# RWKV-7 scan on one core: the triangular inverse on 64x64 diagonal blocks, its last level as corner products, and the tail by four heads

## What is computed

```python
def step(S, inp):
    r_t, w_t, k_t, v_t, kk_t, b_t = inp
    sa = jnp.einsum('bhvk,bhk->bhv', S, -kk_t)
    S = (S * w_t[:, :, None, :] + sa[..., None] * b_t[:, :, None, :]
         + v_t[..., None] * k_t[:, :, None, :])
    y_t = jnp.einsum('bhvk,bhk->bhv', S, r_t)
    return S, y_t
_, y = lax.scan(step, S0, ...)      # 16 heads of 64, 256 steps
```

## Time and profile before

| | us |
|---|---|
| median of three runs | 1625.1 |
| the profiled execution, its own time | 1619.88 |
| its span, first to last instruction | 1618.0 |
| TensorE busy (8756 matmul records) | 1531.3 |
| VectorE busy | 1007.7 |
| ScalarE busy | 684.1 |
| POOL busy | 40.7 |
| mean granted TensorE clock | 0.979 |

### The profile page before, as it was taken

One profiled execution on the slowest core, in us unless ns is written; L12 is line 12 of the kernel. 1 busy time (PEld: TensorE's weight loads), 2 busy tenths in 40 slices (PEclk: granted clock), 3 DMA queues, 4 the chain that ended last, 5 costly groups with the idle time before them and its releaser, 6 DMA issues.

```text
span 1618.0 us, 20860 instructions
## 1 busy us (share of the span) xinstructions
PE 1531.3 (95%) x8756; PEld 1321.3 (82%) x8756; DVE 1007.7 (62%) x1384; ACT 684.1 (42%) x957; POOL 40.7 (3%) x48
## 2 busy tenths in 40 slices
PE   5998998889999989999999999999999999899998
PEld 5777898888888888688888998777888888778887
DVE  6578567565665655757665774266656567566665
ACT  5551100014554454555454434545544443454543
POOL 0010101110000100000000000000000000000000
PEclk9998999899999999999999999999999999999999
DMA  8320000005555543215555655434555554245552
GB/s 291 121 75 27 1 1 1 1 22 212 182 186 196 210 156 105 102 56 182 182 191 199 220 188 184 156 113 174 182 182 192 205 171 146 74 157 188 196 189 79
DMA packets 34942, 230.48 MB, mean 142 GB/s; under 512 B 4208, under 2 KB 4912, under 8 KB 8224
## 3 DMA queue, kind: packets, MB, share of 16 engines
q1 hardware_dynamic: 33040, 223.59, 39.4%
q0 software_dynamic: 1808, 5.56, 1.0%
HBM read 228.07 MB, written 1.05 MB: 142 GB/s over the span
## 4 chain that ended last, share of the span: by engine, by line
PE 85%; DVE 8%; ACT 4%; issue 2%; DMA 0%; SPq 0%; DVEq 0%; ACTq 0%
PE bank L1478 15%; PE bank L1480 15%; PE bank L1479 15%; PE bank L1553 14%; PE bank L1555 7%; PE bank L1772 3%; PE bank L1768 3%; PE bank L1751 3%; DVE wlo L796 2%; ACT whi L399 2%; DVE arena L1141 1%; PE bank L1440 1%; PE bank L1591 1%; DVE arena L997 1%; ACT arena L557 1%
## 5 line engine op out<-in xcount | busy, mean ns | idle before, releaser
L796 DVE TENSOR_TENSOR wlo<-raw,whi 128x2048 fp32r<-128x2048 f32 x208 | 479.2, 2305 | 401.3 <-ACT whi L399 400.8
L399 ACT ACTIVATE whi<-raw 128x2048 fp32r<-128x2048 f32 x208 | 398.6, 1916 | 435.8 <-PE bank L1480 298.8
L1553 PE MATMUL bank<-XHL,whi 128*128 128x512 f32 x1024 | 363.7, 399 | 2.7 <-DVE arena L871 2.1
L1478 PE MATMUL bank<-whi,XHL 128*128 128x512 f32 x896 | 353.1, 394 | 11.4 <-DVE XHL L843 9.4
L1480 PE MATMUL bank<-whi,XHL 128*128 128x512 f32 x896 | 350.1, 391 | 0.0
L1479 PE MATMUL bank<-wlo,XHL 128*128 128x512 f32 x896 | 349.9, 391 | 0.0
L1555 PE MATMUL bank<-XHL,wlo 128*128 128x256 f32 x1024 | 287.6, 281 | 0.0
L1553 PEld LDWEIGHTS bank<-XHL,whi 128*128 128x128 f32 x1024 | 192.7, 188 | 51.2 <-DVE arena L871 3.4
L1478 PEld LDWEIGHTS bank<-whi,XHL 128*128 128x128 f32 x896 | 168.8, 188 | 50.4 <-issue 9.3
L1480 PEld LDWEIGHTS bank<-whi,XHL 128*128 128x128 f32 x896 | 168.8, 188 | 36.3
L1479 PEld LDWEIGHTS bank<-wlo,XHL 128*128 128x128 f32 x896 | 168.9, 188 | 33.9
(11 more groups left out here) (247 smaller groups left out, 1468.8 us busy)
## 6 DMA issues: line engine op xcount, KB each, us to landing
raw<-in_w_mlp SPq DMA_DIRECT2D x128, 1024.0 KB, 4.8
raw<-in_w_rv SPq DMA_DIRECT2D x8, 1024.0 KB, 4.8
raw<-in_w_rg SPq DMA_DIRECT2D x8, 1024.0 KB, 4.8
raw<-in_w_reo SPq DMA_DIRECT2D x8, 1024.0 KB, 4.7
raw<-in_w_k SPq DMA_DIRECT2D x4, 1024.0 KB, 11.6
raw<-in_w_v SPq DMA_DIRECT2D x4, 1024.0 KB, 6.3
raw<-in_w_r SPq DMA_DIRECT2D x4, 1024.0 KB, 4.8
raw<-in_w_rwo SPq DMA_DIRECT2D x4, 1024.0 KB, 4.9
```

Of the source, the lines that this page charges most:

```text
L399: act.activation(whi[:, u % SPLIT_RING], raw[:, u % RAW_RING], ACT.Copy).then_inc(hi_done, 1)
L796: dve.tensor_tensor(wlo[:, u % SPLIT_RING], raw[:, u % RAW_RING], whi[:, u % SPLIT_RING].bitcast(F32), ALU.subtract).then_inc(lo_done, 1)
L1478: pe.matmul(out_, xh[xs], wh[ws], start=start, stop=False)
L1553: pe.matmul(bank[:, :], whi[ws], XHL[:, kt].rearrange("p h t -> p (h t)"), start=(kt == 0), stop=False)
```

## The change

- The scan goes by chunks, not by rounds: the inverse of all 16 heads of a chunk is made at once, for the two 64x64 diagonal blocks of each 128x128 matrix only. `MB`, `X2`, `TI_`, `TT_` and `PM` hold, for lane `f` (first or second head of each of the 8 pairs), the block of tokens 0 to 63 in partitions 0 to 63 and that of tokens 64 to 127 in partitions 64 to 127.
- `prepare(c)`: TensorE makes the blocks and their transposes (64 products of 64x64) and the corner (16); VectorE masks them, POOL makes `TT_` (`first_turn`), ScalarE copies the corner out. No transposes and no ScalarE copy of them any more. `prepare(0)` stands inside the second r chunk, before its fifth step.
- Five levels a chunk (2 to 32). `both` issues, for each of eight pairs, the product of block 0 (array rows and columns 0 to 63) and that of block 1 (rows and columns 64 to 127), both into one bank. VectorE's operations stay 128x512.
- The last level is two products of 64x64 a head (`p1`, `t12`) with ScalarE copies; full inverse columns are put together in `PM[c]`.
- Pair products without the `A` part, 384 columns a head in place of 512, masked in groups of four heads into `M2` (two buffers), and the tail (right-hand side, inverse in two halves, output, keys, state) by four heads, the next group's pair products issued within.
- VectorE's extra work moves: decayed r into levels 0 and 1, the bonus operand into level 2 and its sums into level 4, the split of two `rwo` units into level 3; the normalisations of chunk 0 into the levels of chunk 1 (two or three parts a level), the third one and the fourth behind the last masks.
- The turn of `rwo` uses banks 6, 7, 4, 5.

The core of the diff (masks and buffers, then the queues of ScalarE, VectorE, POOL and TensorE):

```diff
-        M = [at(8240 + 2048 * l, 4, 512) for l in range(2)]
-        TI_ = [at(12336 + 512 * l, 4, P) for l in range(2)]
-        TT_ = [at(13360 + 512 * l, 4, P) for l in range(2)]
-        PM = [at(14384 + 512 * l, 4, P) for l in range(2)]
+        MB, X2, TI_, TT_ = (at(10496 + 1024 * i, 2, KT, HD) for i in range(4))
+        PM = [at(1024, 2, KT, HD), at(8240, 2, KT, HD)]
...
+            for c in range(2):
+                if c == 0:
                     act.wait_ge(bonus_sum, 1)
                     act.activation(bonus, psum[7][:, 0:32], ACT.Copy).then_inc(bonus_read, 1)
+                else:
+                    corner(1)
+                    group_norm(0)
+                    group_norm(1)
+                for f in range(2):
+                    act.wait_ge(p1_prod, 2 * c + f + 1)
+                    act.activation(X2[HD:P, f], psum[f][HD:P, :]...).then_inc(p1_ready, 1)
+                for f in range(2):
+                    act.wait_ge(t12_prod, 2 * c + f + 1)
+                    act.activation(PM[c][HD:P, f], TT_[HD:P, f], ACT.Copy).then_inc(t22_ready, 1)
+                    act.activation(PM[c][0:HD, f], psum[2 + f][0:HD, :]..., scale=-1.0).then_inc(t12_ready, 1)
+                for g in range(4):
...
+                    if c and g == 3:
+                        group_norm(2)
...
+            def prepare(c):
+                for f in range(2):
+                    dve.wait_ge(beta_prod, 2 * c + f + 1)
+                    dve.tensor_tensor(MB[:, f], bank8(4 + f), eight(0), ALU.mult).then_inc(beta_ready, 1)
+                for f in range(2):
+                    dve.wait_ge(turn_prod, 2 * c + f + 1)
+                    step(dve.tensor_tensor(TI_[:, f], bank8(6 + f), eight(2), ALU.mult))
+                    dve.tensor_tensor(TI_[:, f], TI_[:, f], eight(3), ALU.add).then_inc(ti_ready, 1)
+            def level(c, i, work):
+                for f in range(2):
+                    n = 10 * c + 2 * i + f
+                    dve.wait_ge(half_prod, n + 1)
+                    dve.tensor_tensor(PM[c][:, f], bank8(f), eight(4 + i), ALU.mult).then_inc(half_masked, 1)
+                work(i)
+                for f in range(2):
+                    n = 10 * c + 2 * i + f
+                    dve.wait_ge(inv_prod, n + 1)
+                    dve.tensor_tensor(TI_[:, f], TI_[:, f], bank8(2 + f), ALU.subtract).then_inc(inv_doubled, 1)
+                    dve.wait_ge(step_prod, n + 1)
+                    dve.tensor_tensor(TT_[:, f], TT_[:, f], bank8(4 + f), ALU.subtract).then_inc(doubled, 1)
+            def norm_work(i):
+                for r, part in ([(0, 0), (0, 1)], [(0, 2), (0, 3), (0, 4)], [(0, 5), (1, 0), (1, 1)],
+                                [(1, 2), (1, 3)], [(1, 4), (1, 5)])[i]:
+                    group_norm(r, part)
...
+            def first_turn(c):
+                for f in range(2):
+                    pool.wait_ge(beta_ready, 2 * c + f + 1)
+                    pool.tensor_tensor(TT_[:, f], MB[:, f], masks[:, 1:2]..., ALU.mult).then_inc(tt_half, 1)
+                    pool.wait_ge(tt_half, 2 * c + f + 1)
+                    pool.tensor_tensor(TT_[:, f], TT_[:, f], masks[:, 3:4]..., ALU.add).then_inc(tt_ready, 1)
...
-            chunk("r", 1, "feature", 0)
+            chunk("r", 1, "feature", 0, mid=(4, lambda: prepare(0)))
+            def both(bank, w, x, f):
+                for p in range(KT):
+                    for blk in range(2):
+                        rows = slice(blk * HD, (blk + 1) * HD)
+                        ins = pe.matmul(psum[bank][rows, p * HD:(p + 1) * HD], w[rows, f, p], x[rows, f, p],
+                                        start=(p == 0), stop=(p == KT - 1))
+                return ins
...
+                for i in range(5):
+                    for f in range(2):
...
+                        both(f, MB, TI_, f).then_inc(half_prod, 1)
+                    for f in range(2):
+                        n = 10 * c + 2 * i + f
+                        pe.wait_ge(half_masked, n + 1)
+                        if i:
+                            pe.wait_ge(doubled, n - 1)
+                        both(2 + f, TT_, PM[c], f).then_inc(inv_prod, 1)
+                        both(4 + f, PM[c], TT_, f).then_inc(step_prod, 1)
+                for f in range(2):
+                    pe.wait_ge(inv_doubled, 10 * c + 8 + f + 1)
+                    for p in range(KT):
+                        ins = pe.matmul(psum[f][HD:P, p * HD:(p + 1) * HD], X2[0:HD, f, p], TI_[0:HD, f, p],
+                                        start=(p == 0), stop=(p == KT - 1))
+                    ins.then_inc(p1_prod, 1)
+                for f in range(2):
+                    pe.wait_ge(doubled, 10 * c + 8 + f + 1)
+                    pe.wait_ge(p1_ready, 2 * c + f + 1)
+                    for p in range(KT):
+                        ins = pe.matmul(psum[2 + f][0:HD, p * HD:(p + 1) * HD], X2[HD:P, f, p], TT_[HD:P, f, p],
+                                        start=(p == 0), stop=(p == KT - 1))
+                    ins.then_inc(t12_prod, 1)
...
+                pair_products(c, 0)
+                for g in range(4):
+                    G_ = 4 * c + g
+                    pe.wait_ge(pair_masked, 4 * G_ + 4)
...
+                    ins.then_inc(rhs_prod, 1)
+                    if g < 3:
+                        pair_products(c, g + 1)
...
```

More of the change, by code:

```diff
@@ L1182, in _ @@
+            for part in range(6):
+                group_norm(2, part)
             for part in range(3):
@@ new lines, in carried @@
+            def carried(c, g, bank, which):
+                for pp in range(2):
+                    p = 2 * g + pp
+                    pe.matmul(psum[bank][:, pp * P:(pp + 1) * P], AR[:, 2 * p + c, which], S0[:, p],
+                              start=(pp == 0), stop=False)
+            for c in range(2):
+                if c:
+                    prepare(1)
+                for i in range(5):
+                    for f in range(2):
+                        n = 10 * c + 2 * i + f
+                        if i == 0:
+                            pe.wait_ge(ti_ready, 2 * c + f + 1)
+                            pe.wait_ge(tt_ready, 2 * c + f + 1)
+                            pe.wait_ge(corner_ready, 2 * c + f + 1)
+                            if c == 0 and f == 0:
+                                pe.wait_ge(acc_read["act"], READ_COUNT[CHUNK0["r"] + 1][1])
+                        else:
+                            pe.wait_ge(inv_doubled, n - 1)
+                        both(f, MB, TI_, f).then_inc(half_prod, 1)
+                    if c == 0 and i == 4:
@@ L1786, in _ @@
                     if c:
-                        carried(l, p0, 0)
+                        pe.wait_ge(state_ready, 2 * g + 2)
+                        carried(c, g, 4, 0)
                     for h in range(4):
-                        hd = (2 * p0 + h) * HD
-                        ins = pe.matmul(psum[6 + l][:, h * HD:(h + 1) * HD], M[l][:, h, 2 * P:3 * P],
-                                        V[:, c, hd:hd + HD], start=(c == 0 and h == 0), stop=(h == 3))
+                        hd = (4 * g + h) * HD
@@ new lines, in _ @@
+                    ins.then_inc(sa_prod, 1)
+                    if G_:
+                        pe.wait_ge(y_ready, G_)
+                    if c:
+                        carried(c, g, 5, 1)
+                    for h in range(4):
+                        hd = (4 * g + h) * HD
+                        pe.matmul(psum[5][:, h * HD:(h + 1) * HD], M2[g % 2][:, h, 1], V[:, c, hd:hd + HD],
+                                  start=(c == 0 and h == 0), stop=False)
+                    pe.wait_ge(sa_ready, G_ + 1)
```

371 lines of the change are left out of this document (182 added, 189 removed).

## The result

| us | before | changed |
|---|---|---|
| median of four runs | 1623.2 | 1557.5 (1555.2 to 1558.5) |
| the profiled execution, its own time | 1619.88 | 1558.49 |
| its span | 1618.0 | 1556.3 |
| from 129.28 us (the first pair product before the change) to the end of the last output copy | 226.1 | 162.6 |

The ratio is 0.9593, with a 95% interval of 0.9573 to 0.9614: 4.1% faster, 1559 forecast.

What follows compares the result with a forecast made beforehand. TensorE bounds the old scan's doubling levels; with smaller tiles VectorE would. Terms summed to 157.4 us for 226.1; less 2 us for a late normalisation, net 66.7, so 1619.9 to 1553.2, plus 5.2 to the median: 1559, range 1545 to 1613.

Steps and rivals of the forecast that it cites:

- to the first level: From the old scan's start to the first level, through the first preparation and the rest of the r chunk: 10.2 us.
- levels, first half: Five levels: VectorE's 20.5 us, 10.2 of its extra work, the bonus sums' 3.5 and 1.5 for the ends: 35.7 us.
- corners: Two rounds of 16 products, one tile at a time, 3.6 us, plus 1.8 of ScalarE copies standing free: 5.4 us.
- preparation, second half: From group 3 to the second half's first level, nothing covering VectorE's masks and POOL's passes: 4.8 us.
- levels, second half: Five levels with two groups' normalisations between: 20.5 + 10.2 us of VectorE and 2.9 of waits on ScalarE: 33.6 us.
- The price of a record: A weight load and matmul of a 64x64 product in levels and preparations: 0.028 us with two tiles side by side.
- Rivals 1 to 3: One-bank tiles take turns: 1610, chance 0.15; issue limits: about 1590, chance 0.23; fixed price of a record: 1738, chance 0.07.
- VectorE becomes the bound: In the levels: six VectorE operations at 0.69, 4.1 us a level plus extra work; TensorE, 5.4 us, waits behind it.
- The signs that the forecast named: 32 records in 0.9 us, levels of 6.5 to 7.5, VectorE busy for 90%, last output copy near 287 us.
- Wait for the key product: Before the first preparation TensorE idles for 4 us, until the key product L1087 ends at 127.64.
- Groups: Tail by four heads: 6.3 us of TensorE plus 1.0 to 1.1 for five tile shape changes, 7.4 us with state.
- The tail's delay: After the last output: third normalisation late, behind VectorE's last masks and ScalarE's last inverse copy; the fourth starts 2 us later.

Runs made afterwards that it cites:

- e1: Changed kernel with each lane's eight products of the upper left tile issued before the eight of the lower right, instead of alternating; 1644.5 us, ratio 1.0122.
- e6: Changed kernel with the normalisations moved out of the second half's levels into the tail groups of chunk 1; 1569.7 us, ratio 0.9678.
- e4: Changed kernel with ScalarE's square of the third normalisation one group earlier, behind the copy of group 2; 1556.0 us.
- a0: The changed kernel run again without any edit, beside its variants; 1558.95 us, ratio 0.9617.
- e5: Changed kernel with the bonus sums behind the corner products instead of inside level 4, ScalarE's copy of them moved too; 1555.2 us.
- e2: Changed kernel with the first preparation before the seventh step of the last r chunk instead of the fifth; 1555.3 us.

## Why the prediction was right, and where not

By its own steps, the sum of the profile against the one forecast:

| term | forecast | measured |
|---|---|---|
| to the first level | 10.2 | 11.4 |
| levels, first half | 35.7 | 38.8 |
| corners | 5.4 | 5.6 |
| pair products and masks | 3.2 | 4.2 |
| groups, first half | 29.8 | 27.7 |
| preparation, second half | 4.8 | 5.3 |
| levels, second half | 33.6 | 33.7 |
| corners, pair products | 8.6 | 8.9 |
| groups to the last copy | 26.1 | 27.0 |
| sum | 157.4 | 162.6 |
| later output projection | 2 | 3.6 |
| everything behind it | 0 | -1.8 |
| net gain in the profiles | 66.7 | 61.7 |

- **The price of a record was right**, and it carries the result: 0.028 forecast, 0.030 measured. Its derivation (half the columns, half the load, two tiles overlapping) stands: one tile 0.06, two 0.030, four 0.015. Rivals 1 to 3 are out; e1 shows how near the first one was, since the order of two loops is worth 0.018 x 960 = 17 us in each half at full clock and more at half. By the rule of the Trainium skill, TensorEngine Tiling (Array Packing), Restrictions and Gotchas, the two tiles in one bank would have had to take turns; the 0.030 of L1816 speaks against reading it so for tiles that write different partitions.
- **The step that held only in part: "VectorE becomes the bound" of the levels.** It holds for levels 2 and 3 of the first half (7.1 and 8.1 us) and for levels 1 to 3 of the second (7.2, then 5.9 us). It doesn't hold for levels 0 and 1 of the first half, where TensorE's 5.7 us end last, nor for level 4 there and level 0 of the second half, where TensorE is at half clock. Two sizes lie behind this. TensorE needs 5.7 us a level for the 5.4 forecast. VectorE needs less than forecast: its subtractions start 0.60 apart and two masks take 1.35 (3.7 us for the six operations and not 4.1), and the 0.92 of the earlier trace rows is a mean of three operations at 0.68 and one at 1.63 beside POOL; in the levels it took 0.69. So the two engines are nearly even, and e6 takes 7.8 us from VectorE for at most 2. The signs that the forecast named came out accordingly: levels of 5.7 to 8.5 us for 6.5 to 7.5, VectorE at 73 and 86% for 90%, the last output copy at 291.9 for 287.
- **That the second stretch came out at 33.7 for 33.6 is luck.** The forecast has VectorE's 30.7 us and 2.9 of waits on ScalarE. VectorE was busy for 29.05, ScalarE cost it 0.6, and 3.4 were waits for TensorE, nearly all in level 0, at half clock and behind the 0.79 of "issue":

```profile
DVE arena L1132 <- PE bank L1816: 3.0, 4, 2.1
DVE small L1180 <- ACT small L654: 0.6, 2, 0.3
```

The columns of these two rows are the total, the number of waits and the longest. The half clock is not needed for such a length: e4's second stretch took 33.1 us at full clock, with 1.63 of "issue" in level 0 and turns with POOL in levels 0 and 1; a0's took 31.9.
- **Mis-sized: levels of the first half, 3.1 us.** No term stood for half clock, and a piece of 6.9 us at half clock falls on level 4. e5, without such a piece, has 32.1. The bonus sums took 5.2 us there instead of 3.5.
- **Wait for the key product**: 4 us forecast, 4.29 measured. The first preparation then took 5.4 us for 4.5, at half the clock throughout (126.8 to 133.6), 0.9 of the 1.2 us that the stretch was longer. Here two errors offset each other: the forecast priced it at 0.028 a record, but most of it alternates four tiles, which take 0.015, and at full clock it takes 2.96 (e2).
- **Groups**: 7.4 forecast, 7.0 measured. A change of tile shape costs less than the 0.2 taken from the earlier trace rows: L1833 takes 0.63 for 0.43 of work, L1934 1.03 for 0.89, so 0.14 to 0.2 each.
- **The tail's delay**: the mechanism was named (the square behind the last inverse copy) and its size, 2 us, was too small: 3.6. What was left out is that VectorE's passes, once late, fall beside POOL's gate and take turns with it. e4 removes both.
- **Two errors offset each other in the median.** The gain in the profiles was 5 us smaller than forecast. The forecast added 5.2 for a profiled execution that stood below its median (1553.2 + 5.2 is 1558.4, which it gives as 1559); that of the changed kernel stood 1.0 above its own. The 1.5 us between forecast and median are not a measure of the sum's quality; the 5 us are.

## What to carry to other kernels

Price a small-tile product by the time of one tile divided by the tiles that alternate, and write the loops so that neighbouring instructions go to different tiles: here that order alone decided between 4% faster and 1% slower. Once two engines are nearly even in a loop, work taken off one of them brings almost nothing, because the other stands right behind it, so compare both level by level before moving anything. Price a moved operation where it lands, with the instructions that queue behind it and the neighbour that it will run beside.

## What was not expected of the hardware

- TensorE busy without a gap for 80 us with one 64x64 tile at a time stayed at 1.2 GHz (e1, 246.93 to 327.23, granted clock 0.50), where alternating tiles at the same place came back to 2.4 GHz after 3.4 (a0) or 6.8 us. The same order began the first half at full clock and kept it for 40.8 us. The wait of 4.3 us before the first preparation came with half clock in nine traces of nine, and without it there was none in four of four (see e2). What the clock follows is left open.
- Four 64x64 tiles reach 0.015 us a record. In the second preparation TensorE then stands for 1.27 us of "issue" after 124 records, in e2's first one it doesn't; the cause is not shown.
- VectorE's and POOL's elementwise operations take turns by whole instructions: a 0.69 us pass becomes 1.64, a reduction of the same columns stays at 0.67.
- Pieces of 3 to 20 us at half clock differ in length and partly in place from run to run of one text (changed and a0: 6.8 and 3.4 us from 171, 3.4 and 10.2 from 185 and 182). The runs of a0 with the lower mean clock are the longer ones (1555.5 at 0.982, 1563.8 at 0.975), a spread larger than most single edits here.
